# A fused two-block layer on one core: key norms, block inputs and compression placed inside the state loop, state output in halves

## The reference, cut to what matters

```python
h  = rmsnorm(x, norm1_g);  hp = h @ w_in          # u | q | kv | 24 gates | mixer gates
# state mixer: 32 groups x 64 complex states, scan over 256 tokens
y  = Re(C x_t) + d_skip * u;  yg = gelu(y)
y_ssm = yg * sigmoid(yg @ w_glu + b_glu)
# attention mixer: blocks of 32 tokens, stride 16 (15 blocks), per group g and for k and v
hid = gelu((blocks + pe).flatten @ w1);  kc = rmsnorm(hid @ w2), vc = hid @ w2
q, k_selected, k_window = rmsnorm per head of 64
y_nsa = gates * (attention over kc/vc, selected, window)
merged = g0 * (y_ssm @ w_proj_ssm) + g1 * (y_nsa @ w_proj_nsa);  x += merged @ w_out
# then the feed-forward; the second block also needs memory keys/values:
mem_n = rms_norm(mem, mem_norm);  mk, mv = split(mem_n @ mem_w_kv)
```

## Time and profile before

| | |
|---|---|
| device time, median of 3 runs | 1532.83 us (1531.12 to 1534.97) |
| the profiled execution's own time | 1528.67 us |
| its span in the trace | 1526.8 us |
| mean granted PE clock in it | 0.964 |
| PE busy / DVE busy / ACT busy | 1425.8 / 930.8 / 718.8 us |

### The profile page before, as it was taken

One profiled execution on the slowest core, in us unless ns is written; L12 is line 12 of the kernel. 1 busy time (PEld: TensorE's weight loads), 2 busy tenths in 40 slices (PEclk: granted clock), 3 DMA queues, 4 the chain that ended last, 5 costly groups with the idle time before them and its releaser, 6 DMA issues.

```text
span 1526.8 us, 28216 instructions
## 1 busy us (share of the span) xinstructions
PE 1425.8 (93%) x11534; PEld 1379.6 (90%) x11534; DVE 930.8 (61%) x1376; ACT 718.8 (47%) x1180; POOL 196.0 (13%) x211
## 2 busy tenths in 40 slices
PE   5899888779999999999998999999999979899998
PEld 5788777779999999999898999999999977799998
DVE  7997367466654566545775655546565466566544
ACT  8622044344443454545535644536445365554443
POOL 0454200001210011101210111101111010101100
PEclk9999786889999999999999999999999999999999
DMA  8342440144555455554433455554455551245551
GB/s 345 120 141 92 136 133 20 37 157 166 192 188 197 150 187 190 206 193 156 162 139 106 161 187 178 200 195 157 180 186 207 194 193 55 83 166 192 205 187 65
DMA packets 36815, 244.33 MB, mean 160 GB/s; under 512 B 4208, under 2 KB 5360, under 8 KB 8816
## 3 DMA queue, kind: packets, MB, share of 16 engines
q1 hardware_dynamic: 34992, 238.17, 43.8%
q10 hardware_dynamic: 1728, 4.81, 0.9%
HBM read 241.67 MB, written 1.05 MB: 159 GB/s over the span
## 4 chain that ended last, share of the span: by engine, by line
PE 78%; DVE 13%; ACT 5%; issue 2%; DMA 1%; SPq 0%; ACTq 0%; DVEq 0%
PE ps L1785 46%; PE ps L1825 25%; DVE wlo L1007 4%; PE ps L2020 2%; PE ps L1994 2%; ACT whi L573 1%; DVE alo L1372 1%; PE ps L1949 1%; DMA xtok<-in_xt 1%; PE ps L2010 1%; DVE sS L1250 1%; DVE zz L1158 1%; ACT junk L758 1%; ACT pP L719 0%; DVE t L1147 0%
## 5 line engine op out<-in xcount | busy, mean ns | idle before, releaser
L1007 DVE TENSOR_TENSOR wlo<-raw,whi 128x1024 fp32r<-128x1024 f32 (+1 forms) x434 | 506.0, 1208 | 297.3 <-ACT whi L573 297.2
L1785 PE MATMUL ps<-ahi,whi 128*128 128x256 f32 x2112 | 599.7, 284 | 40.1 <-DVE wlo L1007 23.8
L573 ACT ACTIVATE whi<-raw 128x1024 fp32r<-128x1024 f32 (+1 forms) x434 | 427.1, 1032 | 411.6 <-PE ps L1785 217.5
L1785 PE MATMUL ps<-alo,whi 128*128 128x256 f32 x2112 | 595.6, 282 | 0.0
L1785 PE MATMUL ps<-ahi,wlo 128*128 128x256 f32 x2112 | 594.0, 281 | 0.0
L1785 PEld LDWEIGHTS ps<-ahi,whi 128*128 128x128 f32 x2112 | 402.7, 191 | 48.4 <-issue 31.9
L1785 PEld LDWEIGHTS ps<-alo,whi 128*128 128x128 f32 x2112 | 402.2, 190 | 0.7 <-issue 0.7
L1785 PEld LDWEIGHTS ps<-ahi,wlo 128*128 128x128 f32 x2112 | 401.3, 190 | 0.0
L1723 POOL TENSOR_TENSOR hlo<-fh,hhi 128x256 f32 (+3 forms) x104 | 85.9, 826 | 751.7 <-ACT hhi L825 542.3
L1432 DVE TENSOR_TENSOR fa<-ps,r 128x512 f32<-128x512 f32 x104 | 71.9, 691 | 173.8 <-PE ps L1785 173.6
L1825 PE MATMUL ps<-whi,hhi 128*128 128x256 f32 x960 | 147.9, 276 | 0.0
(11 more groups left out here) (339 smaller groups left out, 1409.5 us busy)
## 6 DMA issues: line engine op xcount, KB each, us to landing
raw<-in_w_gu SPq DMA_DIRECT2D x88, 1024.0 KB, 4.8
raw<-in_w_fd SPq DMA_DIRECT2D x44, 1024.0 KB, 4.8
raw<-in_w_up SPq DMA_DIRECT2D x16, 1024.0 KB, 4.8
raw<-in_w_dn SPq DMA_DIRECT2D x16, 1024.0 KB, 4.8
raw<-in_w_ret SPq DMA_DIRECT2D x13, 1024.0 KB, 4.8
raw<-in_w_mg SPq DMA_DIRECT2D x8, 1024.0 KB, 5.3
raw<-in_w_o SPq DMA_DIRECT2D x8, 1024.0 KB, 6.3
raw<-in_w_mem SPq DMA_DIRECT2D x4, 1024.0 KB, 4.9
```

Of the source, the lines that this page charges most:

```text
L573: nc.scalar.activation(whi[:, m % SPL, c], raw[:, n % RAW, c], ACT.Copy).then_inc(S("w_hi"), 1)
L1007: ins = tt(wlo[:, m % SPL, c], raw[:, n % RAW, c], whi[:, m % SPL, c].bitcast(F32), ALU.subtract)
L1785: ins = mm(dst, lhsT, rhs, start=k == 0 and p == 0, stop=k == kt - 1 and p == len(pairs) - 1)
```

## The change

What it does, part by part:

- **Front.** On ACT `turn_tables(0)` moves from before the `whi` of `w_q` 0 to behind that of `w_q` 1, and the `xg` copies move from before `CD` to behind the `whi` that follows `CD`. On DVE the results of `w_u` 1 and `w_q` 0 no longer stand behind the `wlo` of the units two later, and `reduce_angles(1)` moves back.
- **Memory tokens.** ACT scales `yT` by `memg` (eight copies behind `ahead(FILL[3])`); the eight DVE products go; `rm` is applied where the results of `w_mem` are taken out.
- **Block inputs** are written by DVE in tile j = 13, with the two DMAs following; the scratch tiles are laid out so that they lie over state tiles 0 to 7 of the tables. `CP` is 2 x 512 wide with a zeroed tail.
- **Key norms.** ACT, not POOL, squares queries and keys; on PE the transposes of the values and the head sums go between `outputs(6)` and the last fill unit.
- **Compression** stands before the last `outputs(7)`. Blocks are now the stationary side (32 columns, one 32-row quadrant of the result for each of key/value and first/second half of the 16 positions) and the weights the moving side (128 columns). The result is copied by ACT (`cpart`) and two matmuls with identity columns sum the halves and transpose.
- **State output in halves**: gelu, high and low part of feature tiles 0 and 1 before tiles 2 and 3 are there.
- **Behind it** PE does the gate logits and the second compression layer before `w_glu`; `kc_sums` goes between `w_glu` 0 and 1. `kcr` is finished before the `w_ps` units.

```diff
@@ scalar @@
-            turn_tables(0)
             ensure(2, 0)
             act.wait_ge(S("in_tabs"), 16)
             turn_angles(1)
             ahead(AT["w_u", 1])
-            for k in range(KT):
-                ins = scaled_copy(xg, k)
-            ins.then_inc(S("xg"), 1)
+            turn_tables(0)
             act.wait_ge(S("in_bc"), 16)
...
             ins.then_inc(S("cd"), 1)
             ahead(AT["w_q", 0])
+            for k in range(KT):
+                ins = scaled_copy(xg, k)
+            ins.then_inc(S("xg"), 1)
...
             ahead(FILL[3])
+            act.wait_ge(S("in_mem"), 16)
+            for k in range(KT):
+                ins = nc.scalar.activation(yT[:, k], yT[:, k], ACT.Copy, scale=V["memg"][:, k:k + 1])
+            ins.then_inc(S("mem_scaled"), 1)
...
+            act.wait_ge(S("turned"), 2 * N_STATE_TILES)
+            nc.scalar.activation(qsq[:], QK[:], ACT.Square).then_inc(S("qk_squares"), 1)
             act.wait_ge(S("cx"), 1)
...
+            act.wait_ge(S("qk_sums"), 1)
+            nc.scalar.activation(rq[:], PS[6][:, 64:80].rearrange("p (a b c) -> p a b c", a=TT, b=HG), ACT.Sqrt,
+                                 bias=V["eps"], scale=1.0 / DH).then_inc(S("qk_root"), 1)
+            nc.scalar.activation(sdk[:], two(3), ACT.Sqrt, bias=V["eps"], scale=1.0 / DH).then_inc(S("qk_root"), 1)
...
+            state_gelu(0)
+            ensure(SPLIT_BEFORE[AT["w_glu", 0]], AT["w_c1", 1])
+            act.wait_ge(*done(AT["w_c1", 1]))
+            nc.scalar.activation(cpart[:], PS[7][:, 0:P], ACT.Copy).then_inc(S("cmp_part"), 1)
+            act.wait_ge(S("cmp_sum"), 1)
...
+            state_gelu(1)
+            act.wait_ge(S("c_done"), N_STATE_TILES)
@@ vector @@
             scaled(uT[:, 0:2], AT["w_u", 0])
-            reduce_angles(1)
-            scaled(uT[:, 2:4], AT["w_u", 1])
+            tt(uT[:, 2:4], ready(AT["w_u", 1]), over(r[:, 0:T], 2), ALU.mult).then_inc(S("evac"), 1)
...
-            scaled(QK[:, 0:2], AT["w_q", 0])
+            ahead(AT["w_u", 1])
+            reduce_angles(1)
+            tt(QK[:, 0:2], ready(AT["w_q", 0]), over(r[:, 0:T], 2), ALU.mult).then_inc(S("evac"), 1)
...
             turn_inputs(0)
+            ahead(AT["w_q", 0])
...
-                if 5 <= j < 9:
-                    for k in range(2 * j - 10, 2 * j - 8):
-                        stt(yT[:, k], yT[:, k], V["memg"][:, k:k + 1], rm[:, 0:T], ALU.mult, ALU.mult)\
-                            .then_inc(S("mem_normed"), 1)
+                if j == 13:
+                    block_inputs()
+            for k in range(2):
+                state_output(k)
+            dve.wait_ge(S("vv_tr"), 1)
+            cp(VV[:], PS[2][:, :].rearrange("p (a b c) -> p a b c", a=2, b=TT)).then_inc(S("vv"), 1)
+            dve.wait_ge(S("qk_root"), 2)
...
+            state_low(0)
             fill_result(FILL[N_STATE_TILES - 1])
+            for k in range(2, 4):
+                state_output(k)
+            ensure(SPLIT_BEFORE[AT["w_glu", 0]], AT["w_c1", 1])
+            state_low(1)
@@ gpsimd @@
-            pool.wait_ge(S("evac"), GROUP[AT["w_mem", 3]] + 1)
-            tt(yT[:, 0:6], QK[:], QK[:], ALU.mult).then_inc(S("qk_squares"), 1)
-            pool.wait_ge(S("c_done"), N_STATE_TILES)
+            pool.wait_ge(S("qk_sums"), 1)
@@ tensor @@
                 if p:
                     outputs(p - 1)
+                if p == N_STATE_TILES // 2 - 1:
+                    keys_values()
                 fill(FILL[2 * p + 1])
-            outputs(N_STATE_TILES // 2 - 1)
-
-            pe.wait_ge(S("yv"), 4)
...
+            half_j = CMP_STRIDE // 2
+            for j in range(half_j):
+                for half in range(2):
+                    for kv in range(2):
+                        quad, jj = 32 * (kv + 2 * half), j + half_j * half
+                        blocks = CP[:, kv].rearrange("p (m j) -> p m j", j=CMP_STRIDE)
+                        ins = mm(PS[7][quad:quad + 32, 0:P], blocks[:, :, jj],
+                                 raw[:, AT["w_c1", kv] % RAW, jj * P:jj * P + P], start=j == 0, stop=j == half_j - 1)
...
+            outputs(N_STATE_TILES // 2 - 1)
+            pe.wait_ge(S("cmp_part"), 1)
...
+            pe.wait_ge(S("yv"), 2)
...
+            pe.wait_ge(S("yglo"), 2)
+            unit(AT["w_glu", 0], yghi, yglo, GLU_KT)
+            pe.wait_ge(S("kc_sq"), 1)
+            mm(PS[6][:, 96:96 + N_CMP], C["bones"], kcr[:, 1, 0:N_CMP], start=True, stop=True).then_inc(S("kc_sums"), 1)
+            unit(AT["w_glu", 1], yghi, yglo, GLU_KT)
```

More of the change, by code:

```diff
@@ L346, in program @@
         w = [mark]
+        half_turn = 4 * (N_STATE_TILES // 2) * T
+        CP = sb("CP", [P, 2, 2 * T], where=w)
+        CX = sb("CX", [P, 2, T], where=w)
+        VV = sb("VV", [P, 2, TT, P], where=w)
+        assert w[0] == mark + half_turn
         yshi = sb("yshi", [P, 4, T], F32R, where=w)
         yslo = sb("yslo", [P, 4, T], F32R, where=w)
+        assert w[0] == mark + 2 * half_turn
+        qsq = sb("qsq", [P, 6, T], where=[w[0]])
+        at_small = [w[0]]
+        rq = sb("rq", [P, TT, HG, NG], where=at_small)
+        hid = sb("hid", [P, 4, 16], where=at_small)
+        kcr = sb("kcr", [P, 4, 16], where=at_small)
+        VC = sb("VC", [P, HG, P], where=at_small)
+        PC = sb("PC", [P, 2, HG, 32], where=at_small)
+        cpart = sb("cpart", [P, P], where=at_small)
+        w[0] += 4 * 6 * T
+        assert at_small[0] <= w[0]
+        sdk = sb("sdk", [P, 2, T], where=w)
+        assert w[0] == mark + 3 * half_turn
         mrg = sb("mrg", [P, KT, T], where=w)
@@ L690, in _ @@
+            nc.scalar.activation(gate[:], gate[:], ACT.Sigmoid).then_inc(S("gate"), 1)
             for c in range(2):
@@ L695, in _ @@
             nc.scalar.activation(yshi[:], yg[:], ACT.Copy).then_inc(S("yshi"), 1)
[L696 to L699, removed]
+            act.wait_ge(S("kc_sums"), 1)
+            nc.scalar.activation(kcr[:, 2, 0:N_CMP], PS[6][:, 96:96 + N_CMP], ACT.Sqrt, bias=V["eps"], scale=1.0 / DH)\
+              .then_inc(S("kc_root"), 1)
             for c in range(4):
                 ahead(AT["w_ps", c])
[L702 to L707, removed]
             def exps(s):
@@ L1136, in fill_result @@
                     dst = mv[:, c // 2] if c % 2 else mkT[:, c // 2]
[L1137 removed]
+                    bank = ready(n)
+                    if c % 2:
+                        for t in range(TT):
+                            ins = ts(dst[:, t], bank[:, t], rm[:, T + t:T + t + 1], None, ALU.mult)
+                        ins.then_inc(S("evac"), 1)
+                    else:
+                        tt(dst, bank, over(rm[:, 0:T], 2), ALU.mult).then_inc(S("evac"), 1)
                 else:
@@ L1198, in _ @@
+            ins.then_inc(S("gate_logit"), 1)
+            dve.wait_ge(S("kvc_done"), 1)
+            dve.wait_ge(S("nsa_zeroed"), 1)
+            cp(kcr[:, 0, 0:N_CMP], PS[6][:, 64:64 + N_CMP]).then_inc(S("kc"), 1)
+            for i in range(4):
+                ins = cp(VC[32 * i:32 * i + N_CMP, i, :], PS[7][32 * i:32 * i + N_CMP, 64:64 + P])
+            chain(ins)
             ensure(SPLIT_BEFORE[AT["w_glu", 0]] + 1, AT["w_c1", 1])
@@ L1977, in _ @@
                 unit(AT["w_ps", c], yshi, yslo, GLU_KT)
-                if c == 1:
-                    pe.wait_ge(S("kc_sq"), 1)
-                    mm(PS[6][:, 96:96 + N_CMP], C["bones"], kcr[:, 1, 0:N_CMP], start=True, stop=True).then_inc(S("kc_sums"), 1)
             def scores(s):
```

151 lines of the change are left out of this document (69 added, 82 removed).

## The result

| | before | after |
|---|---|---|
| device time, median | 1532.37 us (4 runs) | 1509.18 us (4 runs, 1506.76 to 1511.26) |
| the profiled execution's own time | 1528.67 us | 1510.51 us |
| its span | 1526.8 us | 1508.7 us |
| mean granted PE clock in it | 0.964 | 0.967 |

The ratio is 0.9838, with a 95% interval of 0.9815 to 0.9862: 23.2 us less, where the prediction said 16.8 less. A second timing gave 0.9828 (0.9801 to 0.9855), 26 us less. So the side was right, the size too small: the forecast ratio (1516.0 / 1532.83 = 0.989) lies outside both intervals, and the time stands at the lower end of the range, where rival 1 (1509) was put.

The account below looks back on a forecast made before the run. DVE bounds 38 to 121 us, PE 126 to 162, then small successive steps. -2.9 - 6.4 - 12.6 - 1.9 = -23.8, plus 7.0 for clock, gives -16.8: 1511.9 profiled, 4.2 higher as median, 1516.0 us; range 1508 to 1526.

Parts of the forecast that it names:

- rival 1: The clock holds full speed through the new stretch, so the +7.0 is not paid: -23.8 us, 1509; chance 0.20.
- clock at `w_mg` 0: PE's wait before `w_mg` 0 grows from 2.6 to 3.8 us; a clock fall costs 2.6, 1.6 taken.
- O6 to `w_glu` 0: From the end of `outputs(6)`: transposes and sums 3.5, memory unit and `outputs(7)` 9.0, compression 3.7, gates and second layer 5.0.
- `w_glu`, clock included: Both `w_glu` half units and `kc_sums` take 6.1 us, plus 3.4 for half clock behind the gates.
- tail: Between `w_glu` and `w_ps` 0 the splits, sigmoid and product stay whole, and PE idles 7.4 us.
- clock in `w_ps`: The `w_ps` units, 14.7 us, run slower after a 7.4 us wait: 2.0 us more.
- Front: Up to `w_mg` 0: `inputs(0)` starts at 36.3 instead of 38.33, the first `zin` 2.9 us earlier: -2.9 us.
- Loop: From `w_mg` 0 to `w_mg` 6 the bound goes from DVE to PE, and waits and a slow unit go: -6.4 us.
- Behind the loop: From the end of `outputs(6)` to `w_ps` 0: 34.7 us at full clock against 47.3, so -12.6 us.
- two-quadrant price: Compression priced from `outputs`, where two quadrants alternate: 0.116 us a matmul, 3.7 us for 32.
- clock allowance of +7.0: Time added for half clock in three places: 1.6 us at `w_mg` 0, 3.4 in `w_glu`, 2.0 in `w_ps`.
- Attention: At attention's start scores no longer wait for `kcr`, and DVE's first bias sum comes earlier: -1.9 us.

Follow-up runs that it names:

- e0_again: The changed kernel run again with no edit; median 1506.88 us, ratio 0.9828 to the kernel before.
- e2_yt: The changed kernel with the eight `yT` products back on DVE and plain copies of the `w_mem` results; median 1511.07 us, ratio 0.9843.
- e4_serial: The changed kernel with the same 32 compression matmuls ordered quadrant by quadrant instead of in turn; median 1511.16 us, ratio 0.9839.
- e5_warm: The changed kernel with 15 idle matmuls into an unused bank in PE's wait ahead of `w_ps` 0; median 1506.66 us, ratio 0.9828.
- e8_kcr: The changed kernel with `kcr`'s reciprocal and product back behind the four `w_ps` results; median 1509.71 us, ratio 0.985.
- e3_comp: The changed kernel with compression at its new place in the old form, weights stationary and blocks moving; median 1515.66 us, ratio 0.9889.

## Why the prediction was right in its side and too small in its size

The first value measured is that of the first profile, the second that of e0_again. Both are taken against the first profile of the kernel before.

| step | forecast | measured |
|---|---|---|
| start of `w_mg` 0 | -2.9 | -2.3; -1.5 |
| clock at `w_mg` 0 | +1.6 | +2.8; 0 |
| from there to O6, without that | -6.4 | -6.2 (89.3 to 85.9, less 2.8); -6.0 |
| O6 to `w_glu` 0 | 21.2 us | 18.4; 18.7 us |
| `w_glu`, clock included | 9.5 us | 7.7; 7.4 us |
| tail | 7.4 us | 7.5; 7.5 us |
| clock in `w_ps` | +2.0 | -0.2 (14.5 for 14.7); -0.7 |
| attention's first bias sum, from `w_ps` 0, without the `w_ps` units | -1.9 | -2.0; -2.0 (19.3 - 14.7 before) |

**Front: right, somewhat too high.** The prediction traced `inputs(0)` to within 0.3 us and said that `CD` would be late next; it is, with a wait of 1.87. The first `zin` was 2.3 us earlier, not 2.9, and of the 2.9 us 1.5 to 2.3 arrived at `w_mg` 0, 1.9 on average over all profiles. The wait there was to grow to 3.8 us, as PE would come 4.1 us earlier; PE came 2.1 us earlier (68.67 for 70.74) and waited 2.31.

**Loop: right in its mechanism, its size flattered by the profile it was read from.** The bound went from DVE to PE, all `wlo` waits behind `w_mg` 0 are gone, and so is the slow `w_mg` 6; e2_yt brings both back. The cover on ACT held, and so did that of the block sums: seven of the eight took 0.83 to 0.93 us each with POOL beside them (the first 0.34), 6.3 us in all, and no wait of PE shows for it. But the second profile of the kernel before had its slow unit at 7.41 and O6 at 159.7, so against it the changed kernel gains 2.8 to 4.6 us up to here, not 5.8 to 7.5. Over the three profiles of the old front and loop and the nine of the new, O6 came 5.3 us earlier on average, where the prediction's terms give 7.7 (2.9 + 6.4 - 1.6).

**Behind the loop: right in its order, the compression priced too high.** The two-quadrant price, 0.116 us a matmul, is the second term that was mis-sized. Rows 5 show `outputs` putting two quadrants in turn, and the prediction took that for a layout with four; e4_serial shows that four overlap threefold. 1.7 of the 2.8 us by which the way to `w_glu` was too long are this term (1.99 for 3.7). The estimate from the Trainium skill ("TensorEngine Tiling (Array Packing)", Theoretical Speedup), up to 4x where a dimension is at most 32, gave 1.8 us and was nearer, though the overlap measured is 3.0x. The nearest row differed in just the quantity that the price hangs on.

**The step that failed is the clock allowance of +7.0, in two of its three places.** At `w_mg` 0 it was right as a mean: in the nine profiles that leave front and loop as they are, the unit took 5.89 us three times and 7.3 to 8.7 six times, 1.4 above 5.85 on average, for 1.6 allowed. For `w_glu` it let all 7 us run at 0.52, at 3.4; the clock fell inside it, and it cost 1.6 and 1.3 (7.7 and 7.4 for 6.1). For `w_ps` it added 2.0 for the 7.4 us wait, and the units came out no slower than before (14.5 and 14.0 for 14.7). e5_warm shows that the wait does cost 2.2 to 2.7 us against full clock; the error was to count it as new, when the 14.7 us already held it. Together 5.4 were allowed in these two places, and 0.6 to 1.4 measured.

At attention's first bias sum the forecast stood at 212.4 (229.2 - 16.8), and the two profiles at 207.6 and 205.2. The rows of the table add up to that difference. In the first profile up to O6 it was 1.9 us later than forecast; then the way to `w_glu` was 2.8 shorter, `w_glu` 1.8 and the `w_ps` units 2.2. In e0_again these are 0.2 later, and 2.5, 2.1 and 2.7 shorter. That 1516.0 stood 6.8 above the median of 1509.2 is another sum, with what happened behind attention in it (below).

Rival 1, by which the clock holds, came out right for the stretch up to the gates and wrong behind them. Its number was the nearest in part by luck: at attention's first bias sum it stood at 205.4, and the falls that it left out (1.6 and 1.3 us in `w_glu`, 2.8 and 0 at `w_mg` 0) were made up in part or in full by the way to `w_glu`, which was 2.8 and 2.5 us shorter than its sum.

**Attention: right, and perhaps more came with it.** `kcr` is waited for no longer. From `w_ps` 0 to `w_pn` 0 the time fell from 85.0 and 82.3 to between 79.8 and 81.4, a fall of 0.9 to 5.2 where the sum had 1.9. e8_kcr puts 3.23 us of wait back, and the clock in the start of attention is 0.50 instead of 0.66.

**What stays open.** Up to `w_pn` 0 the profiles give 294.9 and 291.7 us before, and 270.5, 270.1 and 270.3 after. Behind it the first profile after took 6.3 us more than the first before:

```profile
270.00:1508.70 1238.70, 1190.01 (x9918) 1170.77 (x9918) 720.70 (x990) 596.72 (x932) 130.45 (x136) 0.98 0.47 167
1234.00:1244.00 10.00, 6.30 (x26) 5.54 (x27) 8.65 (x12) 6.07 (x13) 0.00 (x0) 0.51 0.31 111
```

The same stretch of the kernel before:

```profile
295.00:1526.80 1231.80, 1183.00 (x9918) 1163.48 (x9918) 720.32 (x989) 596.65 (x932) 130.51 (x136) 0.99 0.47 168
```

The matmuls are the same 9918, and PE was busy 6.9 us longer with them. The difference is clock: by the clock record of the traces PE was at 0.50 for 45.7 us of this stretch in the first profile after and for 31.8 in the first before, 13.9 us more, which cost half of that if PE works through it, 7.0 us. The mark at 1234 is one such fall. Why the clock fell in one execution and not in the other is open: the work is the same.

The profiled executions show gains of 18.2 to 21.9 us (1528.67 to 1510.51 and 1506.74), the timed runs 23 to 26. Both profiled executions of the kernel before (1528.67 and 1528.44) lie 4 to 6 us under the medians of its timed runs, and those of the changed kernel (1510.51, 1507.36, 1506.74) do not. The runs' mean clocks, which are on record, go with this. The two profiled executions of the kernel before had 0.964 and 0.963. Of the 26 runs of it that were timed beside the experiments only three reached 0.963, with 1529.0 to 1531.2 us, and the median was 0.960. The timed runs of the changed kernel had 0.966 to 0.972, its profiles 0.967 to 0.971. A clock lower by 0.004 over 1527 us is worth 6 us (my estimate, if PE works all the time), about what is to be accounted for. So the profile that the prediction was read from was one with fewer falls than most: the 4.2 us carried over to the median basis did not apply to the changed kernel, and on the profiled basis the forecast of 1511.9 was too high by 1.4 to 5.2 us. Where the clock fell in the timed runs can't be seen.

## What to carry to other kernels

Move small steps (block inputs, squares, head sums) under a stretch where PE is the bound, then look at what is left in the tail behind it: here the gates' 3.7 us had been moved away from a wait that they could have filled, and putting them back and halving the tail brought 6 us more. Price an array layout by how many quadrants consecutive matmuls go to, not by the nearest layout in the trace. Before adding a clock fall behind a new wait, look whether the duration taken from the trace already holds one, and judge a removed wait by a mark further on as well. Take a second profile of the kernel before, too: here two profiles of it put the end of `outputs(6)` 2.9 us apart, more than the front was worth on average (1.9).

## What the runs showed of the hardware that I had not expected

- Matmuls of 32 stationary and 128 moving float32 columns cost 0.062 us each when four quadrants take turns and 0.19 us when one quadrant takes eight in a row.
- In e3_comp PE was busy without a gap from 167 to 180 us, at first with float32 matmuls of 30 moving columns, and the granted clock was 1.00 from 167 to 173 and 0.51 from 173 to 180.
- The same wait of 2.3 us before `w_mg` 0 was followed by half clock in two executions of the changed kernel (8.67 and 8.52 us) and not in a third (5.89).
- With nothing changed in it, a stretch of about 1235 us took 1234.6 to 1235.5 us in nine executions, 1238.0 to 1238.3 in four and 1231.9 in one. Between the last and the first profile of the changed kernel (1238.2) the time at half clock in it differed by 13.9 us.
